# A hybrid decoder trunk: the recurrent stage without GpSimd and with interleaved projection tiles, and the attention by query blocks

## What is computed

```python
# layer 0: recurrent block
xb, yb = split(rmsnorm(x) @ w_in + b_in)          # 1024 -> 2 x 1024
gate = gelu(yb)
xc = causal_conv4(xb) + conv_b                     # per channel
r, i = sigmoid(gates(xc))                          # 8 blocks of 128 x 128, for r and for i
log_a = -8 * r * softplus(-lam); a = exp(log_a)
bx = sqrt(-expm1(2 * log_a)) * (i * xc)
hs[t] = a[t] * hs[t-1] + bx[t]                     # scan over the 512 tokens
x = x + (hs * gate) @ w_out
x = x + relu(rmsnorm(x) @ w1) ** 2 @ w2            # 1024 -> 4096 -> 1024
k, v = rmsnorm(x) @ w_kv
# layer 1: differential attention, 8 heads, two score maps a head, keys of 64, values of 128
q = rmsnorm(x) @ w_q
p0, p1 = softmax(q0 k0 / 8 + bias), softmax(q1 k1 / 8 + bias)     # ALiBi, causal
o = (p0 - lam * p1) @ v;  o = rmsnorm_over_128(o) * subln_g * (1 - lam_init)
x = x + o @ w_o;  x = x + the MLP of layer 1;  y = rmsnorm(x)
```

## Time and profile before

| what | value |
|---|---|
| median of 3 runs | 1179.99 us (1178.47 to 1181.94) |
| span of the profiled execution, first to last instruction | 1174.9 us |
| the profiled execution's own time beside its span | not listed apart; the three runs are 3.6 to 7.0 us above the span |
| PE busy | 1108.2 us, 94% |
| DVE, ACT, POOL busy | 653.9, 480.1, 202.2 us |
| mean granted clock of PE | 0.979 |
| recurrent stage, first to last w_out pass | 24.73 to 196.40 us |
| heads 1 to 7 | 620.96 to 775.84 us |

### The profile page before, as it was taken

How to read it: one execution, slowest core, us unless ns; L and a number is a source line. 1 busy time by engine, 2 the same in 40 slices (tenths; PEclk the granted TensorE clock), 3 DMA queues, 4 the chain that set the end, 5 groups by cost and what they waited for, 6 DMA issues and landing times.

```text
span 1174.9 us, 13923 instructions
## 1 busy us (share of the span) xinstructions
PE 1108.2 (94%) x4856; PEld 887.3 (76%) x4856; DVE 653.9 (56%) x937; ACT 480.1 (41%) x745; POOL 202.2 (17%) x141
## 2 busy tenths in 40 slices
PE   8889689999999999999998989889999999999995
PEld 5667568888888888888876656668888888888884
DVE  7997985543443433446467787867533433433434
ACT  6448554422322422434335655745422422422342
POOL 4556733000000000012012242223000000000013
PEclk9989899999999999999999999999999999999998
DMA  5112213222223222232311111113222232222322
GB/s 221 54 54 72 81 48 122 90 90 97 101 90 107 89 97 99 89 108 90 108 54 55 54 53 37 36 54 126 90 98 100 90 107 89 95 102 89 107 72 72
DMA packets 30293, 102.42 MB, mean 87 GB/s; under 512 B 3248, under 2 KB 5552, under 8 KB 30128
## 3 DMA queue, kind: packets, MB, share of 16 engines
q1 hardware_dynamic: 29968, 100.74, 24.9%
q10 hardware_dynamic: 288, 1.18, 0.3%
HBM read 99.81 MB, written 2.10 MB: 87 GB/s over the span
## 4 chain that ended last, share of the span: by engine, by line
PE 78%; DVE 15%; ACT 4%; issue 2%; POOL 1%; DMA 0%; DVEq 0%; SPq 0%; ACTq 0%
PE ps L1251 70%; PE ps L1369 4%; DVE gelu L923 2%; DVE prob L1142 1%; ACT prob L705 1%; PE ps L1432 1%; DVE w_lo L822 1%; DVE lru_v L923 1%; DVE prob L1139 1%; DVE lru_v L949 1%; PE ps L1406 1%; DVE lru_r L985 1%; DVE inv_lam L1137 1%; DVE h_lo L827 1%; DVE lru_v L989 1%
## 5 line engine op out<-in xcount | busy, mean ns | idle before, releaser
L1251 PE MATMUL ps<-u_hi,w_hi 128*128 128x512 f32 x696 | 281.7, 405 | 16.9 <-POOL u_lo L409 12.0
L486 ACT ACTIVATE w_hi<-w_raw 128x1024 fp32r<-128x1024 f32 x184 | 193.5, 1052 | 245.8 <-PE ps L1251 196.8
L1251 PE MATMUL ps<-h_hi,w_hi 128*128 128x512 f32 x704 | 282.5, 401 | 3.5 <-DVE h_lo L827 2.2
L1251 PE MATMUL ps<-h_lo,w_hi 128*128 128x512 f32 x704 | 277.8, 395 | 0.0
L1251 PE MATMUL ps<-h_hi,w_lo 128*128 128x512 f32 x704 | 277.8, 395 | 0.0
L1251 PE MATMUL ps<-u_lo,w_hi 128*128 128x512 f32 x696 | 272.8, 392 | 0.0
L1251 PE MATMUL ps<-u_hi,w_lo 128*128 128x512 f32 x696 | 272.8, 392 | 0.0
L822 DVE TENSOR_TENSOR w_lo<-w_raw,w_hi 128x1024 fp32r<-128x1024 f32 x164 | 204.4, 1247 | 17.7 <-ACT w_hi L486 17.6
L1251 PEld LDWEIGHTS ps<-u_hi,w_hi 128*128 128x128 f32 x696 | 131.4, 189 | 52.8 <-issue 11.3
L1251 PEld LDWEIGHTS ps<-h_hi,w_hi 128*128 128x128 f32 x704 | 134.6, 191 | 35.6 <-DVE h_lo L827 4.1
L1251 PEld LDWEIGHTS ps<-h_lo,w_hi 128*128 128x128 f32 x704 | 134.7, 191 | 28.6 <-issue 1.0
(11 more groups left out here) (174 smaller groups left out, 1010.2 us busy)
## 6 DMA issues: line engine op xcount, KB each, us to landing
w_raw<-weights SPq DMA_DIRECT2D x184, 512.0 KB, 3.2
x<-x_t SPq DMA_DIRECT2D x8, 256.0 KB, 5.4
y_t<-att SPq DMA_DIRECT2D x8, 256.0 KB, 2.3
gelu<-gate_weights ACTq DMA_DIRECT2D x1, 1024.0 KB, 5.7
lam_in<-lam_vecs ACTq DMA_DIRECT2D x1, 128.0 KB, 2.0
vec<-vectors SPq DMA_DIRECT2D x1, 64.5 KB, 1.9
```

The lines of the kernel that those rows point to most:

```text
L486: nc.scalar.activation(w_hi[:, t % RING, :], w_raw[:, t % RAWS, :], ACT.Copy).then_inc(whi_done, 1)
L1251: ins = nc.tensor.matmul(ps[:, bank, :], w[:, slot, ws], o[:, k, :], start=(k == 0 and n == 0), stop=(k == NCH - 1 and n == 2))
```

## The change

Recurrent stage. POOL has none of the stage's work any more: the squares of x go straight to PE, which adds eight float32 matmuls with ones in PSUM (`first_stats`); every `w_lo` of the stage, the product i*xc and the product with the root are DVE's; 1 - r is ACT's; the gate products are one float32 matmul each in place of three float32r passes, so that xc is not split. The bias of xb is folded into a constant (`conv_c`) and the padding, so ACT makes the first tap of the convolution (`tap`) and DVE three. The gelu is one ACT function. The weight tiles of xb and yb are interleaved (`IN_ORDER`), decay, root and scan are done for chunks 0 to 3 while tiles run, then for 4 to 7, and the orders of ACT and DVE are written out. The gate weights are the first DMA that ACT issues, before x and the weights have arrived.

Attention. Each query block is attended on its own, with its transposed probabilities as the stationary operand, so that the output has the queries on partitions. The sub-norm is then a sum along the free axis, on 128 x 4 numbers. Scores are a float32 product in place of three float32r ones. `combined` is three instructions, two of them of one column. The result is scaled on ACT, transposed back (`back`), and split. The loops over the heads are written out. POOL has no work in it.

```diff
+IN_ORDER = ("x0", "x1", "x2", "x3", "x4", "y0", "x5", "y1", "x6", "y2", "x7", "y3", "y4", "y5", "y6", "y7")
...
             nc.scalar.preload_act_table_set("natural_log_exp_and_others")
+            nc.scalar.dma_start(gw[:, :], gate_weights).then_inc(gw_in, 16)
...
+            def tap(m):
+
+                act.wait_ge(bank_read, XT[m] + 1)
+                nc.scalar.activation(lru_v[:, m, :], pad[:, m, PAD:], ACT.Identity,
+                                     scale=col("conv_w", PAD * NCH + m),
+                                     bias=conv_c[:, m:m + 1]).then_inc(tap_done, 1)
...
+            def root(m):
+                act.wait_ge(lru_q, m + 1)
+                nc.scalar.activation(lru_v[:, m, :], lru_v[:, m, :], ACT.Sqrt,
+                                     scale=-1.0).then_inc(sqrt_done, 1)
+                nc.scalar.activation(lru_r[:, m, :], lru_r[:, m, :], ACT.Copy, scale=-1.0,
+                                     bias=1.0).then_inc(lru_a, 1)
+
+            def gelu_of(m):
+                act.wait_ge(bank_read, YT[m] + 1)
+                nc.scalar.activation(gelu[:, m, :], gelu[:, m, :], ACT.Gelu_apprx_tanh,
+                                     bias=col("b_in", NCH + m)).then_inc(gelu_done, 1)
...
+            def squares(h):
+                act.wait_ge(att_mm, QB * (h + 1))
+                for j in range(QB):
+                    ins = nc.scalar.activation(o_square[:, rows(j)], ps[:, BANK_O, rows(j)], ACT.Square,
+                                               accum_out=o_stats[:, h % 2, 0, j:j + 1])
+                ins.then_inc(att_sq, 1)
...
+            def gated_input(m):
+                dve.wait_ge(gates_act, m + 1)
+                nc.vector.tensor_tensor(lru_x[:, m, :], lru_x[:, m, :], lru_v[:, m, :],
+                                        ALU.mult).then_inc(ix_done, 1)
...
+            def scaled_input(c):
+                dve.wait_ge(sqrt_done, c + 1)
+                own.step(nc.vector.tensor_tensor(lru_x[:, c, :], lru_x[:, c, :], lru_v[:, c, :],
+                                                 ALU.mult))
...
             def gates(m):
-                pe.wait_ge(xclo_done, m + 1)
+                pe.wait_ge(conv_done, m + 1)
...
-                    for n, (w, o) in enumerate(((gw_hi, xc_hi), (gw_hi, xc_lo), (gw_lo, xc_hi))):
-                        ins = nc.tensor.matmul(ps[:, bank, :], w[:, ws], o[m % 2],
-                                               start=(n == 0), stop=(n == 2))
+                    ins = nc.tensor.matmul(ps[:, bank, :], gw[:, ws], lru_v[:, m, :], start=True, stop=True)
                 ins.then_inc(gates_mm, 1)
+
+            def first_stats(m):
+                pe.wait_ge(sq_done, m + 1)
+                ins = nc.tensor.matmul(ps[:, BANK_STATS, :], ones[:, :], work[:, m % 4, :],
+                                       start=(m == 0), stop=(m == NCH - 1))
+                ins.then_inc(stat_mm if m < NCH - 1 else stats_done, 1)
...
+            gates_after = {2: (0,), 3: (1,), 4: (2,), 5: (3,), 7: (4,), 8: (5,), 10: (6,), 11: (7,)}
...
-                products = ((kq_hi, kq_hi), (kq_hi, kq_lo), (kq_lo, kq_hi))
...
+                if h and j == 2:
+
+                    pe.wait_ge(olo_done, O_ATT + h)
...
+            def attend(h, j):
...
+                for kb in range(qb + 1):
+                    ins = nc.tensor.matmul(ps[:, BANK_O, qb * P:(qb + 1) * P],
+                                           prob_t[:, j % 2, kb * P:(kb + 1) * P],
+                                           value[:, kb, h * P:(h + 1) * P], start=(kb == 0),
+                                           stop=(kb == qb))
                 ins.then_inc(att_mm, 1)
...
+            def back(h):
+
+                pe.wait_ge(o_scaled, h + 1)
+                pe.wait_ge(trans_read, min(QB * (h + 1) + 2, QB * HEADS))
+                for qb in range(QB):
+                    qs = slice(qb * P, (qb + 1) * P)
+                    ins = nc.tensor.transpose(ps[:, BANK_T, qs], o_rows[:, qs], ident[:, :])
+                ins.then_inc(back_mm, 1)
...
+                part(0)
+                scores(h, 0)
+                if h:
+                    transposes(h - 1, 3)
+                scores(h, 1)
                 part(1)
-                scores(h, i, 2)
+                if h:
+                    attend(h - 1, 3)
                 part(2)
-                transposes(h, i, 0)
+                scores(h, 2)
                 part(3)
-                scores(h, i, 3)
+                transposes(h, 0)
                 part(4)
-                transposes(h, i, 1)
+                scores(h, 3)
+                attend(h, 0)
+                transposes(h, 1)
                 part(5)
-                transposes(h, i, 2)
+                attend(h, 1)
+                if h:
+                    back(h - 1)
                 part(6)
+                transposes(h, 2)
                 part(7)
-                transposes(h, i, 3)
-                attend(h, i)
...
+                attend(h, 2)
```

More of the change, by code:

```diff
@@ L34 @@
 CONV_W = 4
+PAD = CONV_W - 1
 TILE = NCH * P
@@ L85 @@
 RING = 4
-XC = 4
 WARM_UP = 4
@@ new lines, in _ @@
+            split_hi(8)
+            tanh(3)
+            for c in range(0, 4):
+                decay_exp(c)
+            tap(5)
+            split_hi(9)
+            for c in range(0, 4):
+                root(c)
+            split_hi(10)
+            sigmoids(4)
+            tap(6)
+            split_hi(11)
+            tanh(4)
+            sigmoids(5)
+            split_hi(12)
+            tanh(5)
+            tap(7)
+            split_hi(13)
+            sigmoids(6)
+            tanh(6)
+            split_hi(14)
@@ new lines, in _ @@
+            sigmoids(7)
+            split_hi(15)
+            tanh(7)
+            for c in range(4, NCH):
+                decay_exp(c)
+            split_hi(16)
+            for c in range(4, NCH):
+                root(c)
+            split_hi(17)
+            for m in range(0, 6):
+                gelu_of(m)
+            split_hi(18)
+            gated_hi(0)
+            gated_hi(1)
+            gelu_of(6)
+            gated_hi(2)
+            gated_hi(3)
+            gelu_of(7)
+            split_hi(19)
@@ L635, in _ @@
+            for c in range(4, NCH):
+                gated_hi(c)
             nc.scalar.preload_act_table_set("natural_log_exp_and_others")
@@ L785, in _ @@
[L785 to L797 removed]
+                n = (QB - j) * P
@@ L798, in _ @@
+            h = HEADS - 1
+            transposed(h, 3)
+            squares(h)
+            sub_guess_of(h)
+            scaled(h)
+            attended_hi(h)
             residual_step(T_O, N_M1, ("mlp_norm", NCH), early=True)
@@ new lines, in _ @@
+            conv(4)
+            gated_input(3)
+            split_lo(8)
+            decayed(0)
+            branch(5)
+            split_lo(9)
+            for c in range(1, 4):
+                decayed(c)
+            y_scaled(1)
+            conv(5)
+            split_lo(10)
+            scaled_input(0)
+            recurrence(0)
+            branch(6)
+            split_lo(11)
+            scaled_input(1)
+            gated_input(4)
+            recurrence(1)
+            conv(6)
+            y_scaled(2)
@@ new lines, in _ @@
+            split_lo(12)
+            scaled_input(2)
+            gated_input(5)
+            recurrence(2)
+            branch(7)
+            split_lo(13)
+            scaled_input(3)
+            recurrence(3)
+            conv(7)
+            gated_input(6)
+            y_scaled(3)
+            split_lo(14)
+            gated_input(7)
+            y_scaled(4)
+            split_lo(15)
+            for c in range(4, NCH):
+                decayed(c)
+            y_scaled(5)
+            split_lo(16)
@@ L1228, in _ @@
+            h = HEADS - 1
+            variance(h)
+            sub_newton(h)
+            attended_lo(h)
             residual_step(T_O, O_M1, ("mlp_norm", NCH), early=True)
@@ L1451, in output_part @@
                     pe.wait_ge(olo_done, O_ATT + k + 1)
-                    passes(t % RING, t % RING, u_hi, u_lo, k)
-            def head(h, i, first=False, last=False):
+                    ins = passes(t % RING, t % RING, att_hi, att_lo, k)
+                    if k == HEADS - 1:
+                        ins.then_inc(tile_done, 1)
+            pe.wait_ge(olo_done, O_Q + NCH)
+            for part in range(8):
+                kq_part(0, part)
+            pe.wait_ge(bank_read, T_QK)
+            pe.wait_ge(consts_done, 3)
```

852 lines of the change are left out of this document (333 added, 519 removed).

## The result

The changed kernel takes **1161.44 us** (median of 4 runs, 1160.72 to 1162.77) against 1179.23 for the kernel before on the same chip (4 runs, 1178.46 to 1181.94). The ratio is 0.9845, interval 0.9833 to 0.9857: faster by 17.8 us. The forecast was 1138, a gain of 42.0. The time lies just inside the range given, and less than half of the forecast gain came.

A forecast was written before the change was run, and what follows sets the result against it. PE, busy 94% of the span, was taken as the bound. From the span of 1174.9, 22 (start and recurrent stage) and 20 (attention) came off, giving 1132.9; plus 5.1 makes 1138 us, range 1126 to 1162.

The forecast's parts named there:

- the walk: Recurrent stage and attention: engines' written-out lists followed against each other with estimated durations; gains 23 and 21 us.
- The sum for tile 2: Start: seven added products with ones 6.0 us, gate weights' delay 2; tile 2 starts at 29.1, a loss of 4.4.
- its 4 us: Recurrent stage: two stalls lower the clock for some ten passes each, 4 us with the start's.
- The product terms: Start: seven more products with ones at 0.86 us each, 6.0; 17.1 from tile 1's first chunk to tile 2.
- the 4.8 forecast: Recurrent stage: PE stalls 2.5 us at gates(0), behind rstd, and 2.3 at gates(7), behind DVE's list.
- 1142: Recurrent stage: by the skill's drain, eight switches add 11 us on ACT, some 4 reaching PE; the prediction spoke against it.
- two waits left: Each attention head: attend(h,0), its transposed block behind Exps of block 2, 0.4 us; transposes(h,2) for bank T, 0.45.
- the sum for a head: Attention: PE work of 18.2 us a head, 19.0 with waits, against 22.1 before.
- the second rival: Attention keeps a wait of 1.5 us or more a head; it gains 8, time 1150; chance 0.15.
- the two it named: Attention: waiting at bank T (back, attended_hi, attended_lo, then transposes(h,2)), or weight loads that are not hidden.
- 0.04 for both: DVE bounds the recurrent stage and attention keeps its wait of 1.5 us or more a head: 1162; chance 0.04.
- the 5.1 added at the end: Whole kernel: the median of the runs is 5.1 us above the profiled execution's span, added to 1132.9.

The follow-up runs named there:

- both steps: The changed kernel with the gate weights' DMA after chunk 4 of x, and sub-norm newton (DVE) and scaling (ACT) of the head before moved up: 1138.27 us.

## Why the prediction was right in one half and wrong in the other

In spans the forecast was 1132.9 and the trace has 1160.1, 27.2 more. The start and the recurrent stage make 3.7 of it (end of the stage 177.2 for 173.5), the attention 23.7 (201.9 for 198.2 - 20 = 178.2), the rest of the kernel 0.7, and 0.9 goes off because 22 was taken where the walk gave 23.

**The start: right mechanism, term too small.** Tile 2 starts at 31.3, not 29.1, beyond the 31 at which the prediction called itself wrong. The gate weights were entered at 2 us, from the bytes at full share. Removing them from the front gave 4.2. The sum for tile 2 had the delay of a transfer and not what PE's clock does after the wait that the delay makes; 9 passes cost 1.9 us more. The start's slow passes stand only in the stage's sum, inside its 4 us. The product terms held: with the DMA moved, the chain has 17.0 us from tile 1's first chunk to tile 2 (10.62 to 27.59) for the 17.1 of the sum.

**The recurrent stage: right.** 145.9 us from tile 2 to the end, for 144.4, which holds the start's share of the 4 us too. The gates wait twice, 4.4 us for the 4.8 forecast, and `u_lo` 1.9 for 2.1. Taps are 0.75 and scans 1.22 each, everywhere (in the stage POOL does nothing until 149.9), for the 0.78 and 1.19 entered. The Trainium skill (ScalarE: Activation LUTs, What ACT_TABLE_LOAD costs) has a drain of 1.38 us in every switch, by which the prediction made 1142. This trace doesn't agree: none of the stage's eight loads has one, and each starts within 0.03 us of the end of the instruction before. ACT ends an instruction at 68.11, loads from 68.13 and computes at 69.42:

```profile
67.39 0.72 ACT L466 ACTIVATE lru_v<-lru_r,small 128x512 f32<-128x512 f32 x1
68.13 1.28 ACT L471 ACT_TABLE_LOAD   x1
69.42 1.95 ACT L471 ACTIVATE lru_r<-lru_r,small 128x512 f32<-128x512 f32 x3
```

**The attention: the step that failed is the first of the "two waits left", attend(h,0) at 0.4.** PE did stop in the two places named, but at attend(h,0) for 2.5 us. The walk followed the block's own chain (scores, bias, Exp, combined, transpose, attend) and left out what empties the bank that `attend(h,0)` writes: the scaling of the head before, which waits for a guess on ACT and for three small instructions on DVE, and stands on ACT behind the Exps of block 2 and the transposed copy. All of these stood in the change's lists. DVE's three take 0.16 us each, and as work they weigh nothing. As links of a chain, each behind its engine's list, these instructions cost 2.8 us a head: 1.7 of waits and 1.1 of passes at the lower clock (0.95 in the heads), which the sum for a head didn't have. Moving them gave 18.0 between the landmarks.

The other 5.7 are sizes. The two waits cost more than their 0.85 a head: taking them away gave 9.6 us in the traces (183.9 to 174.4), where seven heads have 6.0 of them in the forecast. And the head's work is 18.57 for 18.2, which is 2.6 in seven heads. These two make 6.2, and the 20 us taken was under the walk's 21. In the sum for the work the scores were short. They were entered as 2.35 and their starts show 1.06, 0.84 and 0.63 and some 0.42, 2.95: each of the first three pairs takes 0.20 more than entered. The row that they were read from has such an excess too, 1.42 us where three passes of 512 and three of 384 columns are 1.19. I take it for the change-over. Attending, entered as 2.5, is 2.15, so the 20 weight loads are all hidden.

**The rivals.** What happened is the second rival, an attention that keeps 1.5 us or more of wait a head. But it came by another mechanism than the two it named, and was nearly twice its floor, so its 1150 was too low too. Its chance of 0.15, with 0.04 for both, was low for a list of four engines walked.

**The number that fitted later.** With both steps the time is 1138.27, the forecast's 1138. It is met by errors that cancel. A head still takes 20.1 us and not 19.0, and the attention 183.9 us between the landmarks and not 178.2, 5.7 more. The recurrent half gains 24.8 (statistics at 177.03) and not 22, 2.8 less. And the profiled execution of before was among its fastest: its span stands 4.3 to 5.1 us below the medians of before, that of after 1.3 below its own, so the 5.1 added at the end held some 3 us that were not the launch's but that execution's.

## What to carry to other kernels

For each instruction that PE waits on, ask three questions, not one: when its data are ready, when the bank it writes is empty, and what stands before each link of both chains on its engine. The last is where tiny instructions hide: three of 0.16 us on DVE, and behind them a scaling on ACT, cost nearly the whole forecast of this half, and each engine's order had a part in it. When a change puts a transfer ahead of the first weights, count its delay and the slow passes behind the wait that it makes. After a fix, read the list of waits again before costing the next saving: 5.5 us taken off PE's start were worth 1.6 until DVE's way to the first gates was shortened too.

## What the runs showed of the hardware that was not expected

A stall costs more than its length, and the surcharge isn't steady. Of the eight traces in which PE waits 2.3 us for gates(0), three have four gate records in 1.98 us and 24 passes in 5.5 behind it, 7.4 in all. The other five have 9.1, with the gate records in 2.70 to 3.68. The wait of gates(7), 2.0 long, is the same in nine traces: four have 7.5 behind it and five 9.1 or 9.2, and the clock of the 12 us around it is 1.00 in one and 0.86 in another. So the slow passes cost nothing or 1.7 us a time, with equal code and equal waits. Behind the wait of 3.7 us, seen once, they cost 2.9. Two executions that are alike in the recurrent stage can differ there by 3 us, and a gain of 3 us can't be read from one profile alone. In the heads a wait of 2.5 us in each held the clock at 0.95, and with waits of 0.5 and 0.8 it was 1.00. No length of wait that is safe follows from these rows.

POOL as such costs DVE nothing: 110 memsets, 57.9 us of POOL in a 66.8 us window, left DVE's instructions at their length and the total within 0.6 us, while 40 additions, which read SBUF, cost 23.7 us.
